# Three matrix stages opened by columns, with the roots of their norms spread by TensorE, and another order at the mixers' opening

## What is computed

```
# first block, twice (l = 0, 1)
x = x + 0.5 * swiglu(rms_norm(x, ffn1_norm[l]), ...)      # stages a0, a1
h = rms_norm(x, mix_norm[l]); p = h @ w_in[l]             # stages m0, m1 ("mixers"): stick-breaking,
x = x + merged(attentions(p), sigmoid gates) @ w_out[l]   #   compressed and windowed attention
x = x + 0.5 * swiglu(rms_norm(x, ffn2_norm[l]), ...)      # stages b0, b1

# second block: x and a context of 256 more tokens
h_l = modulate(rms_norm_2(x, g), sh, sc); h_c = modulate(rms_norm_2(ctx, g), csh, csc)
x = x + g_a * y_l;  ctx = ctx + cg_a * y_c                # stage e ("even"): hyena and window attention
x, ctx = ... + g_m * sq_relu_mlp(modulate(rms_norm_2(.)), w1, w2)   # stage p0
x = x + retention_mixer(...)                              # stage o ("odd")
x = x + sq_relu_mlp(...)                                  # stage p1
return rms_norm_2(x, final_g)

def rms_norm_2(x, g):  return x * rsqrt(mean(x * x, -1) + EPS) * g
def modulate(h, shift, scale):  return h * (1 + scale) + shift
```

## Time and profile before

| | us |
|---|---|
| median of 3 runs | 2693.69 |
| lowest, highest | 2693.33, 2693.91 |
| the profiled execution, its own time | 2689.35 |
| its span in the trace | 2687.5 |
| TensorE busy (share of the span) | 2510.4 (93%) |
| VectorE, ScalarE, GpSimd busy | 1658.9, 1179.8, 428.5 |

### The profile page before, as it was taken

How to read it: one execution, slowest core, us unless ns; L and a number is a source line. 1 busy time by engine, 2 the same in 40 slices (tenths; PEclk the granted TensorE clock), 3 DMA queues, 4 the chain that set the end, 5 groups by cost and what they waited for, 6 DMA issues and landing times.

```text
span 2687.5 us, 41648 instructions
## 1 busy us (share of the span) xinstructions
PE 2510.4 (93%) x17737; PEld 2290.9 (85%) x17737; DVE 1658.9 (62%) x2442; ACT 1179.8 (44%) x1900; POOL 428.5 (16%) x387
## 2 busy tenths in 40 slices
PE   8998979999999898899998988899999899998998
PEld 7998868999999896789997765688888799998998
DVE  4786646688887764667776776553342654555653
ACT  5444545544444355555544543342232444344552
POOL 1311015432023000452410120100001011011000
PEclk8999979999999999999999998999999999999999
DMA  7667454576776756346775120132232333334452
GB/s 227 207 225 191 126 159 113 163 229 229 228 235 217 233 130 196 94 127 235 251 269 169 48 75 0 49 109 95 93 108 91 109 94 110 99 106 142 151 194 95
DMA packets 398126, 404.56 MB, mean 151 GB/s; under 512 B 58743, under 2 KB 382611, under 8 KB 397684
## 3 DMA queue, kind: packets, MB, share of 16 engines
q1 hardware_dynamic: 395192, 394.14, 46.8%
q10 hardware_dynamic: 2748, 7.76, 0.8%
HBM read 397.67 MB, written 4.19 MB: 150 GB/s over the span
## 4 chain that ended last, share of the span: by engine, by line
PE 70%; DVE 19%; ACT 6%; issue 2%; DMA 2%; POOL 1%; ACTq 0%; DVEq 0%; SPq 0%; POOLq 0%
PE bank L657 21%; PE bank L659 20%; PE bank L658 20%; DVE rounded L2145 6%; PE bank L665 3%; ACT rounded L1463 3%; DVE plain L2134 2%; PE bank L1402 2%; PE bank L670 1%; DMA plain<-in_w_in 1%; DVE rounded L2191 1%; DVE plain L2366 1%; DVE plain L2155 1%; POOL plain L3067 1%; PE bank L1011 1%
## 5 line engine op out<-in xcount | busy, mean ns | idle before, releaser
L657 PE MATMUL bank<-rounded 128*128 128x256 f32 (+1 forms) x3784 | 1155.5, 305 | 60.3 <-DVE rounded L2191 26.4
L658 PE MATMUL bank<-rounded 128*128 128x256 f32 (+1 forms) x3784 | 1134.6, 300 | 0.0
L659 PE MATMUL bank<-rounded 128*128 128x256 f32 (+1 forms) x3784 | 1133.4, 300 | 0.0
L2145 DVE TENSOR_TENSOR rounded<-plain,rounded 128x1024 fp32r<-128x1024 f32 (+2 forms) x578 | 677.1, 1218 | 508.8 <-ACT rounded L1463 508.5
L657 PEld LDWEIGHTS bank<-rounded 128*128 128x128 f32 x3784 | 734.9, 194 | 110.9 <-DVE rounded L2191 33.9
L1463 ACT ACTIVATE rounded<-plain 128x1024 fp32r<-128x1024 f32 (+2 forms) x634 | 621.9, 1034 | 346.1 <-PE bank L659 284.6
L659 PEld LDWEIGHTS bank<-rounded 128*128 128x128 f32 x3784 | 735.0, 194 | 20.3
L658 PEld LDWEIGHTS bank<-rounded 128*128 128x128 f32 x3784 | 735.7, 194 | 19.3
L657 PE MATMUL bank<-rounded,rounded 128*128 128x256 f32 (+1 forms) x1376 | 421.0, 306 | 30.1 <-DVE rounded L2145 22.7
L658 PE MATMUL bank<-rounded,rounded 128*128 128x256 f32 (+1 forms) x1376 | 417.6, 304 | 0.0
L659 PE MATMUL bank<-rounded,rounded 128*128 128x256 f32 (+1 forms) x1376 | 417.5, 303 | 0.0
(11 more groups left out here) (266 smaller groups left out, 2013.8 us busy)
## 6 DMA issues: line engine op xcount, KB each, us to landing
plain<-in_mlp_w SPq DMA_DIRECT2D x64, 1024.0 KB, 5.2
plain<-in_ada_w SPq DMA_DIRECT2D x48, 1024.0 KB, 5.5
plain<-in_ffn_w_gate SPq DMA_DIRECT2D x44, 1024.0 KB, 5.5
plain<-in_ffn_w_up SPq DMA_DIRECT2D x44, 1024.0 KB, 5.6
plain<-in_ffn_w_down SPq DMA_DIRECT2D x32, 1024.0 KB, 5.1
plain<-in_w_in SPq DMA_DIRECT2D x32, 1024.0 KB, 5.4
plain<-in_od_w_in SPq DMA_DIRECT2D x32, 1024.0 KB, 5.5
plain<-in_ffn_w_down SPq DMA_DIRECT2D x16, 768.0 KB, 5.8
```

What stands on the lines that cost most here:

```text
L657: pe.matmul(dst, a[0], b[0], start=first and i == 0, stop=False)
L658: pe.matmul(dst, a[0], b[1], start=False, stop=False)
L659: ins = pe.matmul(dst, a[1], b[0], start=False, stop=last and i == n - 1)
L2145: dve.tensor_tensor(low, raw, top, SUB).then_inc(*done(("lo", m, half)))
```

## The change

It has four parts.

1. *Roots on columns* (`spread`, `columnroot`, `columnrec`, `broadcast`). The sums of squares are used as the stationary operand with a single column of 1/1024 moving, so that the mean squares of 128 tokens come out as one column, one token a partition. Root and reciprocal then work on 128 x 2. TensorE brings the result back to a row on all partitions by a product of the column, repeated, with the identity matrix, into a bank that the scaling reads.
2. *Turns* (`turn`, into stages p0 and o). The closing unit is computed for the context's columns first, then for x's, each output in a bank of its own; residual, square and sum follow in halves. The opening unit of the next stage is computed the same way (`opening`). The scaling uses four buffers of 256 columns, and odd chunks' low parts are GpSimd's.
3. *Stage e.* The context's h is made during stage b1's steps 22 to 32, by ScalarE and GpSimd; x's h follows after b1. TensorE's mark "begun", which ScalarE awaits before the three loads, stands after the opening.
4. *Mixers.* Four scalings (four buffers) before the weight split; the value product waits chunk by chunk; `flush_one` before chunk 3.

```
+    def spread(s, q, acc, sq, *ready_):
+        b = M.banks[7]
+        ...
+        for tile in range(2):
+            o, ts = b[:, 256 * q + tile:256 * q + tile + 1], slice(128 * tile, 128 * tile + 128)
+            pe.matmul(o, acc[:, ts], ones1024[:, 0:1], start=True, stop=False)
+            ins = pe.matmul(o, sq[:, ts], ones1024[:, 0:1], start=False, stop=True)
+    def broadcast(s, q):
+        b = bank(s, "rstd", q)
+        ...
+        for tile in range(2):
+            ins = pe.matmul(b[:, 128 * tile:128 * tile + 128], M.rcol[:, 2 * q + tile:2 * q + tile + 1].to_broadcast([128, 128]), ident,
+                            start=True, stop=True)
+    def opening(s, m, bs, sums, spreads):
+        for q in (1, 0):
+            cs = slice(256 * q, 256 * q + 256)
+            for k in range(8):
+                if q and k == 2:
+                    sums()
+                if q and k == 5:
+                    spreads()
+                for x in new(at("h", s, k, q)):
+                    pe.wait_ge(*x)
+                for j in range(2):
+                    ins = product(bs[j][:, cs], [(part(m, k, j * 128), hx(k, cs.start, cs.stop))], k == 0, k == 7)
     def even(was):  # TensorE, closing unit
+            if blk == 3:
+                for q in (1, 0):
+                    cs = slice(256 * q, 256 * q + 256)
+                    for j in range(2):
+                        b = bank(s, "wo", 6 + j, q)
+                        for k in order:
+                            if q == 0 and (j, k) == (0, 1):
+                                spread_two(s, 1)
+                            if q == 0 and (j, k) == (1, 5):
+                                broadcast(s, 1)
...
     # ScalarE
+    def opened(s, i, q, c, shift):
+        t, o = M.four[s][i % 4], HSr[:, 0, c, 256 * q:256 * q + 256]
+        ...
+        if c % 2 == 0:
+            act.activation(o, t, ACT.Identity, bias=shift(c, q), scale=1.0).then_inc(*done(("hx", s, c, q)))
+        else:
+            act.activation(t, t, ACT.Identity, bias=shift(c, q), scale=1.0).then_inc(*done())
+            ...
+            act.activation(o, t, ACT.Copy, scale=1.0).then_inc(*done(("hx", s, c, q)))
+    def turn(s, was, shift):
+        square_part(was, 6, 1)
+        square_part(was, 7, 1)
+        columnroot(was, 1)
+        square_part(was, 6, 0)
+        for i in range(16):
+            if i == 3:
+                square_part(was, 7, 0)
+            if i == 5:
+                columnroot(was, 0)
+            opened(s, i, *((1, i) if i < 8 else (0, i - 8)), shift)
     # ScalarE, context(step) of stage b1; GpSimd: ctmp = X * crstd, and the low part from cfull
+        elif step == 23:
+            columnroot("c", 1)
+        elif 25 <= step < 33:
+            c = step - 25
+            for s in new(at("ctmp", c), at("h", "e", c - 2, 1) if c >= 2 else None):
+                act.wait_ge(*s)
+            act.activation(M.cfull[c % 2], M.ctmp[c % 2], ACT.Identity, bias=M.MODS[0][:, c, 1:2],
+                           scale=M.GM[0][:, c, 1:2]).then_inc(*done(("cfull", c)))
+            ...
+            act.activation(HSr[:, 0, c, 256:512], M.cfull[c % 2], ACT.Copy, scale=1.0).then_inc(*done(("hx", "e", c, 1)))
     # VectorE
+    def turn(s, was, weight, shift, add):
+        def part(i):
+            return (1, i) if i < 8 else (0, i - 8)
+        add(6, 1)
+        add(7, 1)
+        columnrec(was, 1)
+        add(6, 0)
+        for i in range(16):
+            if i % 2 == 0 and i:
+                rest(s, i - 2, *part(i - 2), shift)
+            scaled(s, was, i, *part(i), weight)
+            if i == 2:
+                add(7, 0)
+            if i == 5:
+                columnrec(was, 0)
+        rest(s, 14, *part(14), shift)
     def mixer(s, was, l):  # VectorE
+        root(was, M.one.rstd)
+        for c in range(4):
+            times(c)
         lo(U[s, "sq"] + 2)
-        root(was, M.one.rstd)
-        normed(s, was, 256, lambda c, q: col("mix_norm", l * 8 + c))
+        for c in range(0, 8, 2):
+            ...
            dve.tensor_tensor(HSr[:, 1, c, 0:256], M.one.four[c % 4], HSf[:, 0, c, 0:256], SUB)
+            if c < 4:
+                times(c + 4)
+                times(c + 5)
     # GpSimd, stage b1
+            for c in range(8):
+                if c in (2, 5):
+                    for a in ((2, 3) if c == 2 else (4, 5)):
+                        total(s, a, M.one.acc, M.one.sq)
+                context_rest(c)
+                if c < 6:
+                    context(c + 2)
```

More of the change, by code:

```diff
@@ L1118, in even @@
             if jj == 0:
-                for k in range(8):
-                    for x in new(at("h", s, k)):
-                        pe.wait_ge(*x)
-                    for j in range(2):
-                        ins = product(bs[j][:, :], [(part(m, k, j * 128), hx(k, 0, 512))], k == 0, k == 7)
-                ins.then_inc(*done((s, "q", 0), (s, "q", 1), ("unit", m)))
+                opening(s, m, bs, lambda: spread(was, 0, M.one.acc, M.one.sq[1], at(was, "acc", 6), at(was, "sq", 7)),
+                        lambda: broadcast(was, 0)).then_inc(*done((s, "q", 0), (s, "q", 1), ("unit", m)))
+                here(s, "begun", "pe")
                 turned(0)
@@ L1305, in mlp @@
                 ready(m)
-                if half + blk == 0:
+                if half + blk == 0 and l == 0:
+                    opening(s, m, bs, lambda: spread_two(was, 0), lambda: broadcast(was, 0)).then_inc(
+                        *done((s, "w1", 0, 0), (s, "w1", 0, 1), ("unit", m)))
+                elif half + blk == 0:
                     for k in range(8):
@@ L1335, in odd @@
         b_, s = M.od, "o"
-        stage(was)
-        flush(was, 0, 512, M.two.acc, M.two.sq[1])
-        out = {}
         def gate(h, d, half):
@@ L1636, in mixer @@
         root(was, M.one.rstd)
-        normed(s, 256)
+        for c in range(8):
+            for x in new(at(s, "tmp", c)):
+                act.wait_ge(*x)
+            act.activation(HSr[:, 0, c, 0:256], M.one.four[c % 4], ACT.Copy, scale=1.0).then_inc(*done(("hx", s, c)))
         def headsq(name, src, n, free=None):
@@ L2883, in odd @@
         stage(was)
-        root(was, M.two.rstd, 0, 512)
-        normed(s, was, 512, lambda c, q: M.GM[1][:, c, q:q + 1], lambda c, q: M.MODS[1][:, c, q:q + 1])
-        for x in new(L.last()):
-            dve.wait_ge(*x)
         lo(U[s, "k", 0] + 2)
@@ L3116, in even @@
             pool.wait_ge(*x)
-        sums(s, M.two.acc, M.two.sq)
+        for c in range(6):
+            total(s, c, M.two.acc, M.two.sq)
+        turn("p0", s)
         here("end", s, "pool")
@@ L3122, in mlp @@
         stage(was)
-        sums(s, M.two.acc[:, 0:n], [a[:, 0:n] for a in M.two.sq])
+        if l:
+            sums(s, M.two.acc[:, 0:n], [a[:, 0:n] for a in M.two.sq])
+        else:
+            for c in range(6):
+                total(s, c, M.two.acc, M.two.sq)
+            turn("o", s)
         here("end", s, "pool")
```

262 lines of the change are left out of this document (197 added, 65 removed).

## The result

| | before | after |
|---|---|---|
| median of the runs, us | 2693.51 (4 runs) | 2659.32 (4 runs) |
| lowest, highest | 2692.24, 2693.91 | 2652.81, 2659.76 |
| the profiled execution's span | 2687.5 | 2657.4 |
| mean granted clock over it | 0.970 | 0.976 |

The ratio is 0.9868, with an interval of 0.9853 to 0.9884: 34 us or 1.3% less. Forecast were 2660.6 us, so the total was right to 1.3 us. It isn't right term by term, and that the terms' errors cancel is luck. In the traces the changed parts brought 3.4 us more than forecast, the first transfers 3.1 more, and 9.0 us were lost in stages that nobody had edited.

The account below looks back on a forecast made before the run. TensorE, busy 93% of the span, was taken to bound the kernel through its idle time and slow stretches. Terms 18.2 + 6.2 - 1.5 + 10.2 = 33.1 us off the 2693.69 median gave 2660.6 us, range 2648 to 2675.

Parts of the forecast that it names:

- The turns: Even mixer to first MLP and first MLP to odd mixer: closing and opening split by columns, 9.1 us saved each.
- the term for VectorE meeting GpSimd: Turns' openings: VectorE's two-SBUF-input difference collides with GpSimd, adding 0.3 us, so a pair of h parts takes 1.6.
- The base: Turns in the kernel before: start of closing unit to end of opening takes 11.0 + 24.6 = 35.6 us.
- FFN to even: Last FFN to even mixer: opening 13.8, new ScalarE queue wait 4.1, slow products 2.0; 19.9 against 26.1, 6.2 us saved.
- The context in the FFN: Last FFN's third: preparing the context's h there adds work beside VectorE's splits, costing 1.5 us.
- The mixers: Openings of m0 and m1: value products no longer wait for all h; 5.1 us saved each, 10.2 together.
- c_odd's later transfer: Odd mixer: its constants are loaded later relative to the opening; costs nothing, or 1 us if weight transfers slow it.
- The failed step: Whole kernel behind the edits: later work starts by semaphores and freed buffers, so gains stay; no loss counted.
- (a): All hidden: turns 25.6, even's gap without slow stretch, mixers 5.4 each, FFN third 0; 40 us saved, 2654; 14%.
- (b): Full lock in turns, even, mixers and FFN: VectorE waits 0.74 us for each pair; 13 us less saved, 2674; 12%.
- (c): Turns' handover stays late: a root missing its place holds TensorE before the opening, 5 us a turn; 2671; 7%.
- (d): Last FFN: ScalarE's queue, held by GpSimd or the lock, late by 5.8 us in each of eight steps; 2707; 5%.

Follow-up runs that it names:

- Experiment 6: Changed kernel with VectorE's reciprocal in the two turns back on 256 spread columns, behind the spread, instead of 2 before it: 2669.93 us, ratio 0.9911.
- experiment 5: Changed kernel with ScalarE's split and first q copy at the even mixer put ahead of its wait for TensorE's opening and three DMAs: 2654.78 us, 0.9862.
- Experiment 1: Kernel before with the mixers' reordered opening alone, no turns, root columns or new SBUF words: 2678.92 us, ratio 0.9965.
- experiment 4: Changed kernel with the four root columns in unused columns of an existing table, so FFN and MLP hidden arrays keep their old addresses: 2646.78 us, 0.9841.
- the run with 32 words: Changed kernel with 32 words reserved for the root columns in place of 4, moving the arrays behind them: ratio 0.9861.
- the unaltered kernel: The changed kernel as it stands, 2659.32 us, 0.9868; measured again in a later set: 2661.79 us, 0.9884.
- experiment 7: Changed kernel without GpSimd's 16 and ScalarE's 16 passes preparing the context's h in the last FFN (wrong numbers behind it): ratio 0.9873.
- 16 words: Changed kernel with 16 words reserved for the root columns in place of 4: ratio 0.9865.
- 8: Changed kernel with ScalarE's even-mixer order altered, h moved by 192 bytes, 80 words reserved and the first MLP's hidden arrays moved: 2621.86 us, 0.9746.
- experiments 2: Three kernels differing from the changed one only in array places: 32 words reserved 0.9861, 16 words 0.9865, h moved by 64 bytes 0.9788.
- experiment 3: Changed kernel measured again, 2661.79 us, 0.9884; and with h moved by 192 bytes and 16 words reserved, 2628.61 us, 0.9767.

## Why the prediction was right, and where it was not

The mechanism was right in every changed part. The total was right by luck: a loss that it had no term for (9.0 us) nearly cancelled with gains taken too small (3.4 us) and with what the first transfers happened to win (3.1 us). What was left of the miss, 2656.3 forecast for the profiled execution against 2659.35 measured, the medians hide, because the profiled execution of before was 4 us quicker than its median.

- **The turns** (9.1 each; 9.4 and 9.6). The schedule held: first h forecast at T0 + 12.0 and there at 12.0; closing at 12.9, found 12.8; the end at T0 + 26.5, found 25.8. Spread 0.81 us (0.8), root 0.26 and reciprocal 0.17 (0.2 each), broadcast 0.36 (0.5). The 0.7 us too much are the term for VectorE meeting GpSimd, 0.3 a pair: a pair took 1.46 us, not 1.6, and TensorE set the pace, not the feeding. The base was right: from the start of the closing unit to the end of the opening the trace of before takes 35.7 and 35.6 us (35.6 forecast). So over exactly these products a turn gained 9.9 us; the table has 9.4 and 9.6, since its stretches start earlier and hold 0.3 to 0.5 us of the loss by pace. Experiment 6 shows that the chain of roots is as tight as drawn.
- **FFN to even** (6.2; 7.3). Opening 13.1 (13.8 taken), wait 3.75 (4.1), and the slow stretch behind it, about 1.7 (2.0): the six products of 512 columns from 1438.76 on take 2.90 us instead of the 1.36 of six at 0.227, and the rotation ahead of them is a little longer too. Each was a little smaller than its term. The new wait is as named: ScalarE's queue behind the mark of TensorE, shown by experiment 5.
- **The context in the FFN** (-1.5; -0.5, of which the slower pace of the down products can be a part). The wait for splits in this third, 4.6 us from 1350 on before, is 2.1 after, and 2.2 without the passes, so GpSimd's passes beside the splits didn't lengthen them for TensorE.
- **The mixers** (5.1 each; 5.0 and 5.7). m1 was taken as m0, but had 25 slow products after its wait, not 15. Both gaps are 0.46 us rather than none. Experiment 1 shows the term by itself.
- **c_odd's later transfer** (nothing or 1): nothing; the lead stays at 34.6 to 34.7 us through the whole odd mixer.
- **The failed step** is "Everything behind is started by semaphores and buffers that come free, so a gain stays." It left out what a new array does to the addresses of the others. The change's `take(4)` was read for what it holds, not for where it puts everything behind it. Measured: about 9 us of the lead, 7 to 12 by the runs of experiment 4. It was to be seen beforehand only as a question: the trace of before has products of 256 columns at two paces, 120.0 and 113.3 ns, and the forecast took 0.12 for all.
- **The first 60 us** (0; +3.1) are not the change's: the run with 32 words lost 2.8 us of it again with the same instructions, and the second trace of the unaltered kernel 3.0. They lie in the first transfers, and vary between executions. The single run at 2652.81 us isn't profiled, and stays unexplained.

**The rivals.** (a) all hidden, 2654: the parts came to 36.5 us, halfway between the forecast's 33.1 and its 40; without the loss by pace the total would have passed it (43 us under before in experiment 4). (b) a full lock of VectorE and GpSimd at each pair: the lock is real, but in the turns it costs next to nothing, see below. (c) a late handover: no, 0.7 us of slack were left. (d) ScalarE's queue in the FFN: no, experiment 7.

**The lock.** In the turns a scaling reads its root from PSUM and takes 0.48 us beside GpSimd's passes or not. A difference, with two SBUF operands, starts when a GpSimd pass has 0.2 us left, and takes its usual 0.48 as well:

```profile
1712.11 0.74 POOL L3259 TENSOR_TENSOR rounded<-plain,rounded 128x256 fp32r<-128x256 f32 x1 [1.19 <-ACT rounded L1571]
...
1712.67 0.48 DVE L2310 SCALAR_TENSOR_TENSOR rounded<-plain,rounded 128x256 fp32r<-128x256 f32 x1 [0.18 <-ACT rounded L1566]
```

In m0, where scalings and splits read two SBUF operands, GpSimd's pass that starts with VectorE's split takes 3.38 us in place of 0.74, and a scaling that starts in a GpSimd pass 0.96 in place of 0.48:

```profile
242.74 3.38 POOL L3330 TENSOR_TENSOR rounded<-plain,rounded 128x256 fp32r<-128x256 f32 x1 [6.15 <-ACT rounded L1769]
246.08 0.92 POOL L3330 TENSOR_TENSOR rounded<-plain,rounded 128x256 fp32r<-128x256 f32 x1
...
242.82 1.22 DVE L2279 TENSOR_TENSOR rounded<-plain,rounded 128x1024 fp32r<-128x1024 f32 x1
...
245.10 0.42 DVE L2565 TENSOR_TENSOR rounded<-plain,rounded 128x256 fp32r<-128x256 f32 x1
...
246.32 0.96 DVE L2556 SCALAR_TENSOR_TENSOR plain<-plain 128x256 f32<-128x256 f32 x1
```

The ends tell more than the lengths. The scaling ends 0.28 us after GpSimd's pass (247.28 and 247.00), and 0.28 it is for the lengthened scalings and differences of both mixers and of experiment 6's turns too. GpSimd's long pass ends 0.60 us after the third VectorE instruction in a row, the difference of 245.10 that follows the two splits (246.12 and 245.52). So the one that is held waits until the other is through. That holds for the earlier trace rows as well: the difference of 0.76 us ends at 247.48, the GpSimd pass at 247.20. The prediction took it for half a wait; it was a whole one that had begun when the pass was a third over. By the Trainium skill ("SBUF — State Buffer", section "SBUF: two separate sides") the lock is exclusive, held for a whole instruction by whichever starts first, while the other fully blocks. The trace agrees with the blocking; by its records GpSimd's long pass started 0.08 us ahead of the split and was held all the same. What this costs TensorE in m0 is at most the 0.46 us of the gap; no run takes it away. Experiment 6, whose scalings read the root from SBUF, has the collision back in the turn (0.72 us at 1708.27).

## What to carry to other kernels

A few words more in a layout move every array behind them: after each such change compare the pace of TensorE's untouched products, start to start, before any explanation by waits. Where a serial chain on a row of statistics stands between two matrix stages, work on the columns that are ready and keep the statistic one value a token until TensorE has spread it; draw the schedule against the closing work, since slack of 0.7 us was all there was. And when a mark is moved to the end of an engine's work, look at everything that is queued behind it on the waiting engines: reordering that queue gave a further 5 to 6 us.

## What the runs showed of the hardware

**Where the operands start in SBUF changes TensorE's pace.** fp32r products with 128 x 128 stationary operands, granted clock 1.00, mean start to start. The offset is the number of bytes past a multiple of 128 at which the array that was moved (h or a hidden array) starts, counted from the start of the layout; the other operand, a weight unit, lies at offset 0 in all runs:

| offset | 256 columns | 512 columns | seen in |
|---|---|---|---|
| 0 | 120.0 ns | 226.7 ns | h, in before and after; hidden arrays with 16 words, and the first MLP's in 8 |
| 64 | 113.3, 117.8 or a mix | 229 or 233.3 | hidden arrays in before and in experiments 2, 4 and 8; h in 2, 3 and 8 |
| 80 | 119.2 | 234.7 | hidden arrays in after |

The array need not be the moving operand: in the value products it is the stationary one, and 120.0 ns became 113.3 and 117.8. Whether its own start counts or its distance from the other operand is open. What decides between the two values at 64 is open too; the start modulo 256 and modulo 512 bytes were both tried and don't, and within an unbroken run of products the value hardly ever changes (2 of 169 runs in experiment 3). The 120.0 and 226.7 at a multiple of 128 were the same in all runs. The Trainium skill's rule on where an operand may start ("SBUF — State Buffer", section "Operand start alignment") calls itself one of legality, not speed; here the start is worth up to 6% of a product's time, and 37 us of the kernel between 0.9884 and 0.9746, the 6 of ScalarE's order among them.

**A VectorE instruction with two SBUF inputs and a GpSimd pass hold each other up for the whole rest of the earlier one.** The one that is held ends 0.28 us (VectorE) or 0.60 us (GpSimd) after it. If it would have ended later anyway it isn't lengthened, and a scaling with one input in PSUM isn't held (0.48 us beside a pass).

**A reciprocal or root of two columns** costs 0.17 and 0.26 us, against 1.76 for a reciprocal of 256.
